# Masks for the prompt's attention logits added by TensorE, exponentials taken from PSUM, two selection rounds placed later

## The reference

```python
dots = einsum('bthd,bsd->bths', qi, kidx) * 64 ** -0.5
score = einsum('bth,bths->bts', wi, relu(dots))
score = where(arange(n_keys) <= qpos[:, None], score, -inf)
top_val, sel = top_k(score, topk)              # 64 of 256 keys for the prompt, 256 of 1025 for a sample
logits = einsum('btkgd,btskd->btkgs', q, k[sel]) * 64 ** -0.5
logits = where(isfinite(top_val), logits, -inf)
out = einsum('btkgs,btskd->btkgd', softmax(logits), v[sel])
```

## Time and profile before

| | us |
|---|---|
| median of three runs | 841.17 (840.13 to 841.31) |
| the profiled execution, its own time | 843.89 |
| its span | 842.0 |
| PE busy | 790.9 |
| DVE busy | 230.3 |
| POOL busy | 165.8 |
| ACT busy | 117.6 |

### The profile page before, as it was taken

One profiled execution on the slowest core, in us unless ns is written; L12 is line 12 of the kernel. 1 busy time (PEld: TensorE's weight loads), 2 busy tenths in 40 slices (PEclk: granted clock), 3 DMA queues, 4 the chain that ended last, 5 costly groups with the idle time before them and its releaser, 6 DMA issues.

```text
span 842.0 us, 13006 instructions
## 1 busy us (share of the span) xinstructions
PE 790.9 (94%) x5503; PEld 520.7 (62%) x5503; DVE 230.3 (27%) x659; ACT 117.6 (14%) x301; POOL 165.8 (20%) x265
## 2 busy tenths in 40 slices
PE   6999999999999999999997769999999999979965
PEld 4888878888888888885775345853434434432411
DVE  0173216000000000062188770254411210110207
ACT  1020113000000000031222353121110010000110
POOL 3400493444000000004121542003201101100120
PEclk9999999999999999999998868999999999999998
DMA  9799998999621047979324731957999999999991
GB/s 267 269 387 383 364 239 266 297 356 313 224 80 59 0 138 281 281 155 261 123 101 130 260 141 57 410 232 302 368 410 409 397 409 365 396 393 410 392 408 73
DMA packets 112652, 227.44 MB, mean 270 GB/s; under 512 B 25090, under 2 KB 64330, under 8 KB 109396
## 3 DMA queue, kind: packets, MB, share of 16 engines
q1 hardware_dynamic: 96580, 177.13, 59.7%
q0 software_dynamic: 12080, 42.48, 15.1%
q10 hardware_dynamic: 3936, 7.01, 2.3%
HBM read 203.04 MB, written 23.57 MB: 269 GB/s over the span
## 4 chain that ended last, share of the span: by engine, by line
PE 77%; DVE 8%; SPq 7%; DMA 4%; ACT 1%; issue 1%; POOL 1%; DVEq 0%; ACTq 0%
PE ps L723 45%; PE ps L1199 12%; SPq L358 7%; PE ps L1227 6%; DMA slot<-moe_w 3%; PE ps L774 2%; PE ps L1136 1%; DMA slot<-w_in_even 1%; PE ps L1021 1%; PE ps L1073 1%; DVE scr L1840 1%; DVE slot L1851 1%; PE ps L1065 1%; PE ps L899 1%; PE ps L1050 1%
## 5 line engine op out<-in xcount | busy, mean ns | idle before, releaser
L723 PE MATMUL ps<-rw,slot 128*128 128x264 f32 x640 | 142.6, 385 | 0.0
L723 PEld LDWEIGHTS ps<-rw,slot 128*128 128x128 f32 x640 | 120.8, 189 | 21.7
L723 PE MATMUL ps<-xw,slot 128*128 128x264 f32 x512 | 122.9, 396 | 6.4 <-DMA slot<-w_in_even 6.4
L1199 PE MATMUL ps<-slot,hT 128*32 128x512 f32 x1056 | 117.8, 600 | 6.5 <-DMA slot<-moe_w 6.5
L723 PEld LDWEIGHTS ps<-xw,slot 128*128 128x128 f32 x512 | 97.4, 193 | 26.8 <-DMA slot<-w_in_even 8.6
L1199 PEld LDWEIGHTS ps<-slot,hT 128*32 128x32 f32 x1056 | 33.8, 111 | 86.0 <-issue 74.7
L723 PE MATMUL ps<-hT,slot 128*128 128x264 f32 x352 | 79.4, 387 | 0.0
L723 PEld LDWEIGHTS ps<-hT,slot 128*128 128x128 f32 x352 | 66.6, 190 | 12.5 <-DVE xw L1604 1.3
L1227 PE MATMUL ps<-slot,hT 128*32 128x256 f32 x1216 | 68.3, 380 | 1.5 <-DMA slot<-moe_w 1.5
L723 PE MATMUL ps<-yT,slot 128*128 128x264 f32 x256 | 59.5, 388 | 0.0
L1227 PEld LDWEIGHTS ps<-slot,hT 128*32 128x32 f32 x1216 | 38.2, 110 | 27.4 <-DMA slot<-moe_w 2.0
(11 more groups left out here) (438 smaller groups left out, 814.6 us busy)
## 6 DMA issues: line engine op xcount, KB each, us to landing
slot<-moe_w SPq DMA_DIRECT2D x50, 1024.0 KB, 17.2
slot<-moe_w SPq DMA_DIRECT2D x16, 2048.0 KB, 16.0
slot<-ffn_w SPq DMA_DIRECT2D x22, 1024.0 KB, 12.2
scr<-moe_w SPq DMA_DIRECT2D x14, 1024.0 KB, 16.9
slot<-ffn_w SPq DMA_DIRECT2D x8, 1408.0 KB, 6.3
slot<-w_in_even SPq DMA_DIRECT2D x4, 2048.0 KB, 19.7
r_rows<-silu ACTq DMA_DIRECT2D x1, 6528.0 KB, 33.1
slot<-k_pages SPq DMA_DIRECT2D x6, 1024.0 KB, 6.3
```

The costliest lines, as they stand in the source:

```text
L723: mm = pe.matmul(out, lhs(k), rhs(k), start=(k == 0), stop=(k == n - 1))
L1199: mm = pe.matmul(ps[t][32 * j:32 * j + 32, :].rearrange("p (w n) -> p w n", w=2), xgT[:, cap * k + 32 * t:cap * k + 32 * t + 32], moe_slab ...
```

## The change

1. `logits(u)`: ahead of each of the four matmuls stands another, the identity against the mask tile of 128 rows, accumulating in the same bank.
2. The mask tile gets one more instruction at the end of `select`, which multiplies it by -1e30 and posts `shade_done`. `logits(0)` and `logits(4)` wait for it.
3. `masked_logits` becomes `largest`: the row maxima are read from the bank, and L1899 is gone.
4. The exponentials read the bank and write `S`. So `logits(u)` waits for `exp_done` of unit `u - 2` where it waited for `lg_read`, and DVE's wait for `pt_done` goes.
5. Rounds 1 and 2 of tile 1 move from before the last `turn()` to behind `refine(7)`. Rounds 3 to 5 stand in iteration 0 (before: 3 and 4 with L1928), rounds 6 and 7 in iteration 1 (before: 5 to 7), and L1928 stands in iteration 2 with L1932.

```diff
             def logits(u):
...
                     if u >= 2:
-                        pe.wait_ge(lg_read, 2 * (u - 2) + half + 1)
+                        pe.wait_ge(exp_done, 2 * (u - 2) + half + 1)
+                    if half == 0 and c0 == 0:
+                        pe.wait_ge(shade_done, t + 1)
                     for c in range(2):
+                        pe.matmul(out[:, 256 * c:256 * c + L], ident, work[:, t, 0:L], start=True, stop=False)
                         mm = pe.matmul(out[:, 256 * c:256 * c + L],
                                        hT[64 * half:64 * half + 64, QQ + c0 + c, P * t:P * t + P],
-                                       hT[64 * half:64 * half + 64, KK + c0 // 4, 0:L], start=True, stop=True)
+                                       hT[64 * half:64 * half + 64, KK + c0 // 4, 0:L], start=False, stop=True)
...
-                    row_ = S[u % 3][:, half, c, 0:L]
-                    ins = act.activation(row_, row_, ACT.Exp, bias=stat[:, col:col + 1],
+                    row_ = ps[(4, 0)[u % 2] + half][:, 256 * c:256 * c + L]
+                    ins = act.activation(S[u % 3][:, half, c, 0:L], row_, ACT.Exp, bias=stat[:, col:col + 1],
...
+                    V.tensor_scalar(dst, dst, NEG, None, ALU.mult).then_inc(shade_done, 1)
...
-                if i in (6, 7):
-                    select(1, (range(0, 1), range(1, 3))[i - 6])
+                if i == 6:
+                    select(1, range(0, 1))
...
-            def masked_logits(u):
-                t = u // 4
-                L = P * (t + 1)
-                if u >= 3:
-                    dve.wait_ge(pt_done, 2 * (u - 2))
+            def largest(u):
+                L = P * (u // 4 + 1)
                 for half in range(2):
                     dve.wait_ge(lg_done, 2 * u + half + 1)
...
-                    link(V.scalar_tensor_tensor(
-                        out=dst, in0=work[:, t:t + 1, 0:L].to_broadcast([P, 2, L]), scalar=NEG,
-                        in1=src[:, :].rearrange("p (c s) -> p c s", c=2)[:, :, 0:L],
-                        op0=ALU.mult, op1=ALU.add))
-                    V.tensor_reduce(out=stat[:, col:col + 3:2], in_=dst, axis=AX, op=ALU.max,
-                                    negate=True).then_inc(lg_read, 1)
+                    V.tensor_reduce(out=stat[:, col:col + 3:2],
+                                    in_=ps[(4, 0)[u % 2] + half][:, :].rearrange("p (c s) -> p c s", c=2)[:, :, 0:L],
+                                    axis=AX, op=ALU.max, negate=True).then_inc(lg_read, 1)
...
             refine(7)
+            select(1, range(1, 3))
             for u in range(8):
                 if u < 6:
-                    masked_logits(u + 2)
+                    largest(u + 2)
                 if u < 7:
                     shares(u + 1)
                 if u == 0:
-                    select(1, range(3, 5))
+                    select(1, range(3, 6))
+                if u == 1:
+                    select(1, range(6, 8))
+                if u == 2:
                     link(V.tensor_scalar(eqk, X, kth, 0.0, ALU.is_equal, ALU.add, accum_out=sst[:, 4:5]))
-                if u == 1:
-                    select(1, range(5, 8))
-                if u == 2:
                     link(V.tensor_tensor_scan(junk, eqk, eqk, 0.0, ALU.add, ALU.bypass))
```

More of the change, by code:

```diff
@@ L294, in build @@
         chosen, counted, passes_ready = sem("chosen"), sem("counted"), sem("passes_ready")
+        shade_done = sem("shade_done")
         sel_ready, sel_done, sel_copied = sem("sel_ready"), sem("sel_done"), sem("sel_copied")
@@ L1885, in _ @@
                     select(0, range(2 * i - 6, 2 * i - 4))
-                if i in (6, 7):
-                    select(1, (range(0, 1), range(1, 3))[i - 6])
-            def masked_logits(u):
-                t = u // 4
-                L = P * (t + 1)
-                if u >= 3:
-                    dve.wait_ge(pt_done, 2 * (u - 2))
+                if i == 6:
+                    select(1, range(0, 1))
+            def largest(u):
+                L = P * (u // 4 + 1)
                 for half in range(2):
                     dve.wait_ge(lg_done, 2 * u + half + 1)
-                    dst = S[u % 3][:, half, :, 0:L]
-                    src = ps[(4, 0)[u % 2] + half]
                     col = 4 * (u % 4) + half
-                    link(V.scalar_tensor_tensor(
-                        out=dst, in0=work[:, t:t + 1, 0:L].to_broadcast([P, 2, L]), scalar=NEG,
-                        in1=src[:, :].rearrange("p (c s) -> p c s", c=2)[:, :, 0:L],
-                        op0=ALU.mult, op1=ALU.add))
-                    V.tensor_reduce(out=stat[:, col:col + 3:2], in_=dst, axis=AX, op=ALU.max,
-                                    negate=True).then_inc(lg_read, 1)
+                    V.tensor_reduce(out=stat[:, col:col + 3:2],
+                                    in_=ps[(4, 0)[u % 2] + half][:, :].rearrange("p (c s) -> p c s", c=2)[:, :, 0:L],
+                                    axis=AX, op=ALU.max, negate=True).then_inc(lg_read, 1)
             def shares(u):
@@ L1912, in _ @@
             own = top[:, 0, :]
-            masked_logits(0)
+            largest(0)
             refine(6)
             radix(7)
-            masked_logits(1)
+            largest(1)
             dve.wait_ge(own_done, 1)
```

## The result

The changed kernel took 861.58 us (four runs, 861.27 to 873.45) against 841.24 us; the ratio is 1.0262, with an interval of 1.0231 to 1.0293 (the bare medians give 1.0242). I had forecast 839.0, in a range of 835.0 to 843.0, with a chance of 0.17 for slower.

A forecast was written before the change was run, and what follows sets the result against it. The end of the samples' attention, which holds back the expert weights, was taken as the bound. Walking that stage put the output projection at 520.1 instead of 522.26, so 841.17 - 2.2 = 839.0 us, range 835.0 to 843.0.

The forecast's parts named there:

- Prices: Costs taken from profile rows: logits units 1.75 us in tile 0, 3.5 in tile 1; exponentials 0.11 us less each.
- step 4: `logits(4)` waits for `shade_done` of tile 1 until 477.0; `exps(3)` ends at 482.3 instead of 479.4, 2.9 us behind.
- Step 2: From `logits(0)` to `exps(1)`: 0.65 us longer than 14.6, with full clock back before `k_logits`; `exps(1)` ends at 469.9.
- slower: the clock falls before `logits(4)`: Rival, chance 0.18: PE idles some 3 us for `shade_done`, half clock adds 3.5 to 5 us, total 842.5 to 844.
- Step 5: Tile 1 units turn in a loop of PE and ACT, 5.3 us each; `exps(5)` ends at 492.9, level with before.
- eaten: Rival, chance 0.30: the new waits, or exponentials or clock falling short, eat the gain, about 841 us.
- Step 1: Front: two rounds leave, 1.96 us less, 0.2 more for the multiplication; `logits(0)` starts at 454.7 instead of 456.5.
- Steps 6 and 7: DVE's iteration 4 takes 4.4 us from `shares(5)`, `smax_done` at 497.3; then 3.3 us to the end of `exps(6)`, 500.6.
- the factor of 1: A microsecond won or lost at the end of the attention arrives at the kernel's end one for one.
- Step 8: From `probs_t(6, 0)` to the output projection: old order, 18.2 us, so 520.1 instead of 522.26, 2.2 us earlier.
- better: Rival, chance 0.12: TensorE keeps full clock from `logits(0)` through the tail, 834.5 to 835.5 us.

The follow-up runs named there:

- e2_idle128: Kernel before plus a 128-row identity matmul, its result overwritten, ahead of each logits matmul, no waits changed: 853.03 us, ratio 1.0114.
- e8_filled: Changed kernel plus two 512-column matmuls, result not used, in PE's gap before `logits(0)`: 860.03 us, ratio 1.0244.
- e11_idle_wait: Kernel before plus overwritten 128-row identity matmuls, with PE waiting for `exp_done` instead of `lg_read`: 854.83 us, ratio 1.0151.
- e1_rounds: Kernel before with part 5 alone (selection rounds and L1928 moved, masks still added by DVE): 837.49 us, ratio 0.9924.
- e3_idle64: Kernel before plus overwritten identity matmuls on the same 64 rows as the logits matmul behind each: 845.10 us, ratio 1.0032.
- e9_wait: Kernel before with one edit, PE waits for `exp_done` where it waited for `lg_read`: 841.85 us, ratio 0.9995.
- e10_both: Kernel before with part 5 alone, plus two 512-column filling matmuls before `logits(0)`: 834.79 us, ratio 0.9911.
- e13_no_shade: Changed kernel with tile 1's identities reading constants instead of the mask, so `logits(4)` doesn't wait for `shade_done`: 852.20 us, ratio 1.0114.

## Why the prediction was wrong

**The step that failed** is the price in "Prices": "With an identity of all rows in front of each, I assume that nothing overlaps: eight full matmuls, 1.75 us in tile 0 and 3.5 in tile 1". I took the loss of the overlap between halves for the whole cost. The rows of L829 had 128-row matmuls among their like, where loads hide; between 64-row matmuls each of the eight also shows its weight load. Measured: 3.3 and 5.0 us. My lower bound was 2.9 for tile 1; I set no upper one above 3.5 at full clock. By itself, with the longer stretch at half clock behind it, this costs about 10 us (e2_idle128). Nearly as much, 9.4 us, came with the wait for `shade_done` (step 4). The wait was in my sum; the low clock behind it was put at nothing there and stood only as a rival, at 3.5 to 5 us.

**Step 2**, "I let the clock come back before `k_logits`": it came back at 469.8, after both units and most of `k_logits`. `logits(0)` and `(1)` took 11.6 us, not 5.2. Filling the gap lets them run at full clock, and what that gains in the end is too small to be told (e8_filled), as the clock then falls later. In e11_idle_wait it stayed at half for 17 us in the same way. What goes with it is the change of rows: this first stretch at half clock lasts 13.7 to 20.5 us in the profiles of the seven kernels whose units change rows and start behind the gap, and 3.4 to 10.2 us in the four without (before, e1_rounds, e3_idle64, e9_wait), of which e3_idle64 has as many matmuls. Each of the long stretches ends inside `k_logits`. Why the change of rows keeps the clock low is open.

**Step 4** was right in its mechanism and wrong in its size. `shade_done` came 3.2 us after `shares(2)`, forecast 2.9 (L1846 took 0.89, twice its row). What followed was 9.2 us of logits, not 3.5. My rival "slower: the clock falls before `logits(4)`" happened to the letter and was priced at 3.5 to 5 us; with the true price of the matmuls, wait and clock make 9.4, about half each. I gave as a reason against it that 7 us of logits would bring the clock back; the clock came at 500.5, behind the 9.2 us of `logits(4)`, three small groups and the first identity of `logits(5)`. The Trainium skill's warning of idle gaps ("TensorE: Matmul & The Clock Gate", "Why this matters for your kernels") agrees with these rows, where PE idled for 4.28 us; the fall in e8_filled, with no pause ahead of it, is not covered by it.

**Step 5**: the loop of PE and ACT is what sets the pace, as forecast, at 7.3 to 7.7 us a turn instead of 5.3: 1.5 from the matmuls, the rest in small amounts from transposes and hand-overs, and the exponentials gained 0.05 us each (0.36 from start to the accumulator's read, against 0.41), not 0.11. My row for that, a Relu without a row sum, was not like enough; ACT by shape in the changed kernel, against 498 ns in the earlier trace rows:

```profile
...
L1469 ACT ACTIVATE scr<-ps,fin 128x256 f32<-128x256 f32 x4 | 1.8, 480 | 0.0
...
```

The wait for `exp_done`, which I blamed in the rival "eaten", is free (e9_wait) and costs 1.8 us at the new price.

**Step 1 and part 5** were right in kind and too small: moving the rounds gains 5.1 us alone, not 1.96. Its profile has the clock at half for 6.8 us in the front where the kernel before has 10.2, and full again at 502.3 instead of 509.5. That the clock gives the rest is argued from this and from its eight runs, whose times go with their clocks, and isn't isolated: e10_both, which holds the clock in the front, is 2.7 us lower, with overlapping intervals.

**Steps 6 and 7 and the factor of 1** held: `smax_done` is 4.5 us after `shares(5)` (forecast 4.4), `exps(6)` end 3.6 behind that (3.3), and the end moved with the stage. **Step 8** kept the old length of the tail, 19.5 us from `exps(6)`; it took 17.1, as it ran at full clock. That is what the rival "better" had priced at 2 to 3 us, and it hid a part of the loss.

By the medians the parts add up to 842.5 + 10.4 (rows changed) + 1.8 (`exp_done`) + 9.4 (`shade_done`) - 4.3 (rounds) = 859.8 of 861.6. The last 2 us are not placed. The 9.4 is itself a difference from the changed kernel; what the sum tests is the others, 850.4 against the 852.2 of e13_no_shade. With each run taken against the kernel before on its own chip the parts are 10.4, 2.2, 11.3 and -2.9, in sum 21.0 where 20.3 was measured, so each is known to about 2 us. DVE's relief, the point of taking the masks off it, shows nowhere in the changed kernel: it idled 1.7 to 2.4 us before each of `shares(3)` to `shares(6)`.

## What to carry to other kernels

A matmul's price depends on its neighbours: before adding one, look whether it covers the same rows of the array as those around it, and price it from a row with such neighbours or bound it by the load's own duration as well. If shapes must mix, group them. Work that waits for another engine in a TensorE-bound loop cost twice here, once as the gap and once as the clock behind it, and cheap matmuls in that gap took back 4 to 5 us. In the gap in front of the stage what they bring was too small to be told, so try each place by itself. Split a change into its parts before judging it: the half that helped here was hidden under one that lost more than four times as much.

## What the runs showed of the hardware

- Going from float32 matmuls over 128 rows to ones over 64 rows, or back, costs about 0.2 us at full clock and 0.3 at half for each change, whether 128 or 256 columns follow (0.42, 0.63; 0.72, 1.15). Matmuls that stay on 64 rows take 0.43 to 0.54 us for 256 columns (e3_idle64), with their loads 0.2 us ahead. The Trainium skill ("TensorE: Matmul & The Clock Gate", Part 3) says that a weight load overlaps matmuls in flight only where the row groups differ; identity and logits matmul share row groups, and the exposed loads agree with that. But matmuls on equal rows share them too, and theirs run ahead: over 128 rows in a stream (0.22 us each), over 64 in e3_idle64. So what the rows here show is a price of changing rows, not of sharing them. The same part also lets a load be pulled ahead when it goes to a background weight buffer; whether that is what equal rows use no run here shows.
- TensorE stayed at half clock for 17 us, over some 11 us of such matmuls and 4.0 to 5.5 us of `k_logits`, although its busy share was 99% (the changed kernel, e2_idle128, e11_idle_wait). With as many matmuls on 64 rows it was at half for 3.4 us (e3_idle64). In e8_filled it fell from full to half with PE busy for 9 us without a pause. A full busy share neither brought the clock back nor held it; what does stays open.
- A float32 exponential with a row sum takes 480 ns from PSUM and 498 from SBUF for 256 columns; the read of the sum behind it takes 0.21 us against 0.19.
